# A two-block transformer on one core: first projections from the unnormalised input, convolution from PSUM, values ahead of logits, merged sums kept in PSUM

## The reference, cut to what matters

```
h     = rmsnorm(x, ln_mix_pre)                      # x * rs(token) * gain(feature)
proj  = h @ w_in
qkv   = silu(depthwise_conv5(proj[q,k,v of GDN]))   # 5 taps over tokens, 3*1024 channels
q, k  = l2norm(q), l2norm(k)                        # 8 heads of 128
g, b  = decays and betas from 32 gate columns
o_a   = rmsnorm(delta(q,k,v,g,b) + reversed delta) * silu(z)
o_b   = dilated window attention, 3 groups x 4 heads, joined by softmax over groups
merged= sigmoid(ga) * (o_a @ w_branch_a) + sigmoid(gb) * (o_b @ w_branch_b)
x     = x + rmsnorm(merged @ w_out);  x = x + rmsnorm(relu(rmsnorm(x) @ w_ff1)**2 @ w_ff2)
```

## Time and profile before

| | |
|---|---|
| median of 3 runs | 2108.91 us (2108.44 to 2112.96) |
| the profiled execution | 2110.14 us |
| its span | 2108.3 us |
| TensorE busy | 1998.5 us, 95% |
| VectorE, ScalarE, GpSimd busy | 940.0, 743.6, 614.7 us |
| TensorE's share of the chain that ended last | 86% (DVE 7%, ACT 4%) |
| mean granted clock | 0.972 |

### The profile page before, as it was taken

How to read it: one execution, slowest core, us unless ns; L and a number is a source line. 1 busy time by engine, 2 the same in 40 slices (tenths; PEclk the granted TensorE clock), 3 DMA queues, 4 the chain that set the end, 5 groups by cost and what they waited for, 6 DMA issues and landing times.

```text
span 2108.3 us, 25286 instructions
## 1 busy us (share of the span) xinstructions
PE 1998.5 (95%) x10748; PEld 1607.1 (76%) x10748; DVE 940.0 (45%) x1549; ACT 743.6 (35%) x1235; POOL 614.7 (29%) x206
## 2 busy tenths in 40 slices
PE   6998899999999999999999999998999999999997
PEld 3777899999977787778778888887766548766456
DVE  4797455656522221303336403514534664434663
ACT  4674232221433322322233212223343553343551
POOL 2431211222432322334424444442423002423001
PEclk8999799999999999999999999998999999999999
DMA  4121000000233322322222222221312002212001
GB/s 170 60 80 60 1 1 2 2 1 1 95 120 105 106 90 76 111 84 91 89 80 82 98 100 100 100 99 61 130 60 80 1 1 83 90 60 80 1 1 40
DMA packets 29001, 142.01 MB, mean 67 GB/s; under 512 B 2871, under 2 KB 7351, under 8 KB 14808
## 3 DMA queue, kind: packets, MB, share of 16 engines
q1 hardware_dynamic: 18944, 123.27, 16.5%
q10 hardware_dynamic: 9944, 17.12, 2.5%
HBM read 135.13 MB, written 5.24 MB: 67 GB/s over the span
## 4 chain that ended last, share of the span: by engine, by line
PE 86%; DVE 7%; ACT 4%; issue 1%; DMA 0%; POOL 0%; SPq 0%; POOLq 0%; DVEq 0%; ACTq 0%
PE bank L398 48%; PE bank L942 13%; PE bank L599 4%; PE bank L409 3%; PE bank L1800 3%; PE bank L1821 3%; PE bank L1807 2%; DVE WK L868 2%; PE bank L957 2%; PE bank L1275 1%; DVE WK L887 1%; PE bank L1251 1%; PE bank L1749 1%; ACT WK L1930 1%; ACT w_part L356 1%
## 5 line engine op out<-in xcount | busy, mean ns | idle before, releaser
L398 PE MATMUL bank<-x_part,w_part 128*128 128x512 f32 x3360 | 786.7, 394 | 3.5 <-ACT WK L1497 3.0
L398 PEld LDWEIGHTS bank<-x_part,w_part 128*128 128x128 f32 x3360 | 633.1, 189 | 141.5 <-issue 9.0
L2240 POOL TENSOR_TENSOR w_part<-RAW,w_part 128x2048 fp32r<-128x2048 f32 (+1 forms) x90 | 403.3, 4484 | 780.1 <-ACT w_part L356 777.7
L942 PE MATMUL bank<-WK 128*128 128x64 f32 (+1 forms) x2336 | 281.2, 277 | 3.4 <-DVE WK L1088 1.6
L942 PEld LDWEIGHTS bank<-WK 128*128 128x128 f32 x2336 | 275.7, 195 | 4.3 <-DVE WK L1088 1.8
L2240 POOL TENSOR_TENSOR w_part<-WK,w_part 128x2048 fp32r<-128x2048 f32 (+1 forms) x30 | 126.2, 4206 | 376.5 <-ACT w_part L356 376.5
L356 ACT ACTIVATE w_part<-RAW 128x2048 fp32r<-128x2048 f32 (+1 forms) x90 | 166.4, 1850 | 173.9 <-PE bank L398 138.3
L398 PE MATMUL bank<-f_part,w_part 128*128 128x512 f32 x768 | 174.4, 389 | 0.0
L398 PEld LDWEIGHTS bank<-f_part,w_part 128*128 128x128 f32 x768 | 144.2, 188 | 29.9
L868 DVE SCALAR_TENSOR_TENSOR WK<-WK,COL 128x512 f32<-128x512 f32 x96 | 101.7, 1060 | 3.4
L1009 ACT ACTIVATE WK<-bank 128x256 f32<-128x256 f32 x80 | 31.0, 388 | 200.9 <-PE bank L957 200.6
(11 more groups left out here) (257 smaller groups left out, 2372.6 us busy)
## 6 DMA issues: line engine op xcount, KB each, us to landing
RAW<-wts SPq DMA_DIRECT2D x84, 1024.0 KB, 4.8
WK<-wts SPq DMA_DIRECT2D x24, 1024.0 KB, 4.8
WK<-scratch ACTq DMA_DIRECT2D x16, 256.0 KB, 2.7
RAW<-wts SPq DMA_DIRECT2D x6, 512.0 KB, 3.3
WK<-wts SPq DMA_DIRECT2D x6, 512.0 KB, 3.2
scratch<-WK ACTq DMA_DIRECT2D x4, 768.0 KB, 3.3
WK<-xT SPq DMA_DIRECT2D x4, 512.0 KB, 7.1
WK<-xT ACTq DMA_DIRECT2D x1, 2048.0 KB, 11.1
```

Source lines behind the costliest of these rows:

```text
L398: mm = pe.eng.matmul(b[:, :], W[w][:, k, c:c + P], src[x][k], start=start and k == 0 and n == 0, stop=stop and k == kn - 1 and n == 2)
L942: mul = lambda o, a, b: E.matmul(o, a, b, start=True, stop=True)
L2240: eng.tensor_tensor(low_part(i), raw_part(i), high_part(i).bitcast(F32), ALU.subtract).then_inc(w_split, 1)
```

## The change

Four places are rewritten.

- **Front.** VectorE first forms x * gain alone, in two parts (`UX`, called `gained_part`), as x arrives. TensorE takes the four tiles of chunk 0 from it, in pairs: the high weight piece by both parts, then the low piece. The row factor rs is multiplied into these four banks afterwards (`rowed`, in place). The gate projection moves behind tile (1, 0). ScalarE rounds weight piece 0 before the norm's Ln, piece 1 after its Exp and piece 2 behind the second rounded activation tile. The gate weights are loaded behind weight piece 0. On the engines the gates' small steps come about two tiles later.
- **Convolution.** `XP` is gone. ScalarE writes the middle tap times its weight to `CV`, and VectorE adds four taps read from the bank, 510 or 511 wide; the bank is free only then.
- **Dilated order.** The first value projection stands before the first two logits, and the third and fourth logits before the first `av`, behind the transposes of the values. VectorE copies the values before it handles the third logits.
- **Merge.** The stage barrier on TensorE goes, with explicit waits in its place. ScalarE takes the first two sigmoids inside the dilated stage. The products with WB and the sum stay in the bank; rounding and subtraction read the bank, and the subtraction of tile i - 1 stands behind the sum of tile i.

```diff
 def act_norm(...):
+            ahead(upto=1)
             for k in range(KO):
                 ...
                 act.eng.activation(XH[0][:, k, :], norm_mem(nm)[2][:, k % 2, :], ACT.Copy)...
+                if k == 1:
+                    ahead(upto=2)
 def load_pe():
             pe_norm("n1")
+            for p in range(2):
+                bs = [job(("qkv", 0, 2 * p + j)) for j in range(2)]
+                hi, lo = (w.rearrange("p (k n) -> p k n", n=256) for w in (high_part(p), low_part(p)))
+                pe.wait_ge(*at(("hi", p)))
+                for k in range(KO):
+                    pe.wait_ge(*at(("ux", k)))
+                    for j, b in enumerate(bs):
+                        for x in range(2):
+                            pe.eng.matmul(b[:, :], hi[:, k, j * P:(j + 1) * P], UX[x][:, k, :], start=k == 0 and x == 0, stop=False)
+                pe.wait_ge(*at(("split", p)))
+                for j, b in enumerate(bs):
+                    for k in range(KO):
+                        mm = pe.eng.matmul(b[:, :], lo[:, k, j * P:(j + 1) * P], UX[0][:, k, :], start=False, stop=k == KO - 1)
+                    mm.then_inc(*pe.did(("pe", ("qkv", 0, 2 * p + j))))
+                used(p)
 def load_act():
-            act_norm("n1", XT, need=arrived, before_sum=lambda: ahead(upto=1))
+            act_norm("n1", XT, need=lambda k: [(x_in[k // 2], 16)], before_sum=lambda: ahead(upto=0))
 def load_dve():
+            for k in range(KO):
+                dve.wait_ge(x_in[k // 2], 16)
+                g = col("ln_mix_pre", k)
+                dve.eng.tensor_scalar(UX[0][:, k, :], XT[:, k, :], g, None, ALU.mult).then_inc(*dve.did())
+                dve.wait_ge(*dve.last())
+                dve.eng.scalar_tensor_tensor(out=UX[1][:, k, :], in0=XT[:, k, :], scalar=g, in1=UX[0][:, k, :].bitcast(F32),
+                                             op0=ALU.mult, op1=ALU.subtract).then_inc(*dve.did(("ux", k)))
 def qkv_pe():
-            for c in range(6):
+            for c in range(1, 6):
                 for i in range(4):
-                    fm(("qkv", c, i), f"A{c}", i * P, HTS)
-                    if c == 0 and i == 1:
+                    fm(("qkv", c, i), f"A{c}", i * P, HTS, **(dict(need=lambda k: ("n1", "h", k)) if c == 1 and i == 0 else {}))
+                    if c == 1 and i == 0:
+                        gates_project_pe()
+                    if c == 1 and i == 1:
                         gates_turn_pe()
-                    if c == 1 and i == 0:
+                    if c == 1 and i == 3:
                         gates_sum_pe()
-                    if 1 <= c <= 4 and i == 1:
+                    if 1 <= c <= 4 and i == (2 if c == 1 else 1):
                         sums(c - 1)
 def qkv_act():
-                act.eng.activation(XP[:, n % 2, 2:S + 2], ps(("qkv", c, i))[:, :], ACT.Copy)\
-                    .then_inc(*act.did(("xp", n), free=("qkv", c, i)))
+                act.eng.activation(CV[:, n % 2, :], ps(("qkv", c, i))[:, :], ACT.Copy, scale=col("conv", n * CONV + 2))\
+                    .then_inc(*act.did(("cv", n)))
 def qkv_dve():
+            def rowed(i):
+                dve.wait_ge(*at(("pe", ("qkv", 0, i))))
+                V.tensor_tensor(ps(("qkv", 0, i))[:, :], ps(("qkv", 0, i))[:, :], RSB, ALU.mult)...
-                V.tensor_scalar(cv, XP[:, n % 2, 0:S], wc(0), None, ALU.mult).then_inc(*dve.did())
-                for j in range(1, CONV):
-                    dve.wait_ge(*dve.last())
-                    V.scalar_tensor_tensor(out=cv, in0=XP[:, n % 2, j:j + S], scalar=wc(j), in1=cv, ...
+                for j, (to, at_, m) in ((0, (2, 0, S - 2)), (1, (1, 0, S - 1)), (3, (0, 1, S - 1)), (4, (0, 2, S - 2))):
+                    if j:
+                        dve.wait_ge(*dve.last())
+                    V.scalar_tensor_tensor(out=cv[:, to:to + m], in0=x[:, at_:at_ + m], scalar=wc(j), in1=cv[:, to:to + m], ...
+                                           free=("qkv", c, i) if j == CONV - 1 else None))
 def dil_pe():
+                project(hh, "v", 0)
                 for label in [("bqk", hh, g) for g in range(6)]:
                     pe.wait_ge(*at(label))
                 logits(n)
                 logits(n + 1)
-                for g in range(3):
-                    project(hh, "v", g)
+                project(hh, "v", 1)
+                project(hh, "v", 2)
                 turn(n)
                 turn(n + 1)
-                logits(n + 2)
                 ...
+                logits(n + 2)
+                logits(n + 3)
                 for t in range(TT):
                     pe.wait_ge(*at(("bvc", hh, t)))
                 av(n)
-                logits(n + 3)
                 av(n + 1)
 def dil_act():
+            for i in range(2):
+                act.wait_ge(*at(("pe", ("GA", 0, i))))
+                A.activation(SG[:, i, :], ps(("GA", 0, i))[:, :], ACT.Sigmoid)...
+            ahead("GA0", 0)
 def merge_pe():
-            pe.stage("merge")
+            pe.stage("merge", barrier=False)
 def merge_act():
-                    act.eng.activation(MG[0][:, 4 * half + i, :], TM[:, i, :], ACT.Copy)...
+                    act.eng.activation(MG[0][:, 4 * half + i, :], ps(("WB", half, i))[:, :], ACT.Copy)...
 def merge_dve():
+            def low(half, i):
+                dve.wait_ge(*at(("mgh", half, i)))
+                V.tensor_tensor(MG[1][:, 4 * half + i, :], ps(("WB", half, i))[:, :], MG[0][:, 4 * half + i, :].bitcast(F32), ALU.subtract)...
-                    V.tensor_tensor(SG[:, i, :], ps(("WB", half, i))[:, :], SG[:, i, :], ALU.mult)...
-                    V.tensor_tensor(TM[:, i, :], TM[:, i, :], SG[:, i, :], ALU.add)...
-                for i in range(4):
-                    ...
-                    V.tensor_tensor(MG[1][:, 4 * half + i, :], TM[:, i, :], MG[0][:, 4 * half + i, :].bitcast(F32), ALU.subtract)...
+                    V.tensor_tensor(m, m, SG[:, i, :], ALU.mult).then_inc(*dve.did())
+                    dve.wait_ge(*dve.last())
+                    V.tensor_tensor(m, m, TM[:, i, :], ALU.add).then_inc(*dve.did(("mg", half, 1, i)))
+                    if i:
+                        low(half, i - 1)
+                low(half, 3)
```

More of the change, by code:

```diff
@@ L628, in build @@
         GF = wk(19712, S)
+        UX = parts("gained_part", 22784, KO, S)
         def load_pe():
@@ L829, in qkv_act @@
                 act.wait_ge(*at(("pe", ("qkv", c, i))))
-                act.wait_ge(*at("xpzero"))
+                if not c:
+                    act.wait_ge(*at(("rowed", i)))
                 if n >= 2:
-                    act.wait_ge(*at(("conv", n - 2)))
-                act.eng.activation(XP[:, n % 2, 2:S + 2], ps(("qkv", c, i))[:, :], ACT.Copy)\
-                    .then_inc(*act.did(("xp", n), free=("qkv", c, i)))
+                    act.wait_ge(*at(("si", *tiles[n - 2])))
+                act.eng.activation(CV[:, n % 2, :], ps(("qkv", c, i))[:, :], ACT.Copy, scale=col("conv", n * CONV + 2))\
+                    .then_inc(*act.did(("cv", n)))
                 if i % 2:
@@ L856, in qkv_dve @@
             dve.stage("qkv")
[L857 to L869 removed]
+            RSB = norm_mem("n1")[1]
@@ L1397, in dil_act @@
                         bias_tiles(r)
-                for r in range(2):
-                    prob(n + r)
-                    bias_tiles(n + r + 2)
                 if not hh:
@@ L1412, in dil_act @@
                         ahead(f"Bv{hh}", (g - 1) * 2 * P)
+                    else:
+                        for r in range(2):
+                            prob(n + r)
+                            bias_tiles(n + r + 2)
                 moves(n)
@@ L1420, in dil_act @@
             moves(15)
+            for i in range(2):
+                act.wait_ge(*at(("pe", ("GA", 0, i))))
+                A.activation(SG[:, i, :], ps(("GA", 0, i))[:, :], ACT.Sigmoid).then_inc(*act.did(("sg", 0, 0, i), free=("GA", 0, i)))
+            ahead("GA0", 0)
         def dil_dve():
@@ L1484, in merge_pe @@
                 for nm, src in (("GA", HTS), ("WA", tiles_of(OAT, KO)), ("GB", HTS), ("WB", tiles_of(OBT, 4))):
+                    if nm == "WA" and half == 0:
+                        pe.wait_ge(*at(("end", "zgate", "act")))
+                        pe.wait_ge(*at(("end", "zgate", "dve")))
+                    if nm == "WB" and half == 0:
+                        pe.wait_ge(*at(("end", "dil", "dve")))
                     for i in range(2 if nm == "GA" and half == 0 else 0, 4):
@@ L1492, in merge_act @@
                 for m, nm in enumerate(("GA", "GB")):
-                    for i in range(4):
+                    for i in range(2 if not m and not half else 0, 4):
                         act.wait_ge(*at(("pe", (nm, half, i))))
@@ L1504, in merge_act @@
                     act.wait_ge(*at(("mg", half, 1, i)))
-                    act.eng.activation(MG[0][:, 4 * half + i, :], TM[:, i, :], ACT.Copy).then_inc(*act.did(("mgh", half, i)))
```

(5 more changed lines are left out.)

58 lines of the change are left out of this document (29 added, 29 removed).

## The result

The changed kernel takes 2061.03 us (median of 4 runs, 2060.73 to 2062.03), the kernel before 2108.77 us (4 runs, 2108.44 to 2112.96). The ratio is 0.977, its 95% interval 0.9753 to 0.9787. The profiled execution of the changed kernel took 2060.84 us with a span of 2059.0; the one of before had 2108.3.

The account below looks back on a forecast made before the run. TensorE was taken to bound the kernel, with stops and half-rate clock to remove. Front 27.2, dilated order 16.6 and merge 6.4 sum to 50.2, from 2110.14 to 2059.9; the runs' median 1.2 lower gave 2059, range 2050 to 2075.

Parts of the forecast that it names:

- the way to the second sums: Front, up to the end of the second chunk's sums: about 91.3 us instead of 111.92, -20.6.
- the periods: Front's steady part, four tiles each: 26.64 us falls to 23.7; two periods give -5.9.
- The start: Front: TensorE starts chunk 0 at about 15.9 us, after the first weight piece's high part.
- The wait near 60 us: Front: TensorE waits 4.4 us from about 61, for the convolution of tile (1, 0) at 65.3.
- bound "without any fall 22.9": Front, up to the second chunk's sums: gain of 22.9 instead of 20.6 if the clock never falls.
- the range of the parts: Whole kernel: 2052 to 2069 us, from the bounds of the front, dilated stage and merge.
- The tail: End of the front: one last convolution takes 2.9 us instead of 3.6, -0.7.
- The mechanism of the front: Convolution taps: two SBUF operands wait for GpSimd's whole instruction, a bank and one SBUF operand do not.
- rival A: Convolution: taps from a bank still wait for GpSimd, periods stay 26.6, 5.9 and 4 lost, 2069 us; chance 8%.
- The dilated order: Dilated stage, k to next q: 30.8 and 32.1 us become 27.3, twice each, -16.6.
- Rival B: Dilated stage: the clock falls in each hh behind the transposes, 4 x 1.7 us, 2066; chance 10%.
- The merge: Merge: -4.5 us from the first sigmoids' stop and its clock fall, -1.9 at the end, together -6.4.

Follow-up runs that it names:

- the taps alone: The changed kernel with the old front, chunk 0 again projected from the normalised input, taps still read from the bank: 2072.7 us.
- the start alone: The changed kernel with ScalarE copying each tile to SBUF and the four taps reading and adding there, chunk 0 still early: 2083.94 us.
- three such orders on ScalarE: The changed kernel with gate steps behind the last square, values' last rounding behind probability copies, merged parts' roundings before the next weight piece: 2053.46 us.

## Why the prediction was right, point by point

The forecast was 2059, range 2050 to 2075; it came to 2061.03. The sum of 50.2 stands against 49.3 in the span. It hides two mis-sized terms, the way to the second sums and the periods, and that they cancel is luck.

- **The start.** Forecast 15.9, by the first weight rounding; it was 17.07, by the norm's row sums, which stand ahead on TensorE and last 10.03. I had not looked at who releases whom there. In the other profiled executions with this start those sums take 8.6 to 10.1, and chunk 0 starts between 15.75 and 17.4. The gate parts were ready before GpSimd's first subtraction, so VectorE met two of them and not three and the last activation part was ready at 40.6, not 42.3.
- **The wait near 60 us and the way to 91.3.** The wait was to end at 65.4, by ScalarE, and ended at 66.0, by ScalarE. It lasted 2.1 and not 4.4 because TensorE came to it at 63.9 and not at 61: a later start, and three sums of 0.86 each where I had counted half. From there I had 0.4 for the last sum, two falls of the clock at 1.7, gate sums 4 and the chunk's sums 1.7; measured were 1.13, no fall, 2.6 and 3.5. Hence 89.75 and -22.2 instead of -20.6. The missing falls are luck: four of the seven profiled executions have both, two have one. The bound "without any fall 22.9" covers it, but the terms as written give 20.6 + 3.4 = 24.0. The same care was missing in the range of the parts: their bounds give 2053.7 to 2070.4, not 2052 to 2069.
- **The periods: the step that failed.** I took "1.7 of sums" for a period, half of what they cost. Four sums take 3.43 (0.86 each, two passes of 0.43). So the period of before, 26.64, held a stop of 1.4 and not 3.1; the new period is 25.24, and two give -2.8 instead of -5.9. The tail: -0.6 for the rest of the stage. Front: 25.6 at the last tile, 27.2 forecast.
- **The mechanism of the front** was right in that taps on a bank don't wait for GpSimd (748 ns; I had taken 692). But the text reads as if the start were the gain and the taps worth 5.9. The two experiments show 13.8 for the taps alone, and 2.6 for the start alone. Had rival A (the taps still wait) been true, the cost, going by the kernel with the taps from SBUF, would have been up to 23, not the 10 I gave it: 2084, outside my range.
- **The dilated order.** -16.6 forecast, -15.9 measured. 27.52 per hh against 27.3; the bank behind ScalarE's rounding was next late, as forecast, and taking it away gave the 26.9 of bare work. Rival B is out: by the rule of the Trainium skill ("TensorE: Matmul & The Clock Gate", "Part 4: PE-mode transpose") `av` would run at half clock behind the transposes; it took 2.68 for 24 in each hh, and the granted clock is 1.00 from 636 to 645 us.
- **The merge.** -6.4 forecast, -7.1 at the end of the projection and -6.2 with the slower L547. The low parts came at 997.6, 999.5 and 1001.5, which is 1045.1, 1047.1 and 1049.0 with the 47.5 between the two kernels there added; forecast were 1045.2, 1047.4, 1049.5. I had taken 1.9, between 1.1 (the work) and 2.8 (with the fall of the clock); it was 2.8: 1.4 for the six matmuls that now lie inside the stop, and the fall of before, which is gone. The first stop gave 2.9 and, in this pair of profiles, 1.45 of clock.
- **Waiting for GpSimd.** That a VectorE step with two SBUF inputs waits for GpSimd, and one with a bank and an SBUF input does not, is shown three times over: 7.36 against 3.12 for four taps in one kernel, 6.10 for eight taps beside GpSimd, 4.61 against 0.69 for the subtraction. The Trainium skill, "SBUF — State Buffer", "SBUF: two separate sides", names the same condition for its exclusive lock, two SBUF inputs; these rows agree, and in them an output in SBUF doesn't count: the taps and the low parts are written there.
- **Not foreseen:** -1.6 at the bias rows, +0.9 at L547, both clock, both in code that the change leaves alone.

## What to carry to other kernels

Ask of an earlier start who can keep up with it: with VectorE waiting for GpSimd, 20 us of head start were worth 2.6, and 11.7 once a tap read its bank. Then price a rival as a whole run, with every meeting of the two engines, not as the stop it brings back once. And when a stop is left, look for what stands ahead of the late step on its own engine; three such orders on ScalarE gave 7.9 us more. Last, before calling a stage's gain measured, look at more than one execution: here the same front ended anywhere between 89.75 and 93.2.

## What the runs showed of the hardware

- A VectorE step with one operand in a bank and a scalar from a column of SBUF takes 0.75 (L901, and L725 at 0.75 with both operands in SBUF); with an immediate scalar it takes 0.69 (L1474). I had priced the taps by the immediate one.
- An in-place VectorE product or sum on a bank takes 0.69 to 0.70 (L889, L1573, L1575), and ScalarE can round from the same bank right behind it.
- The clock falls or does not behind the same stop, in the same code. A stop of 2.1 was followed by full clock in one execution and by 0.64 in another; a stop of 2.97 by 143.2 for 624 matmuls in one kernel and 141.7 in the other. Behind the stop of 2.1, six of seven profiled executions show a fall. Most falls cost 1.3 to 1.7, the one at 1004.9 us with the joining sums in SBUF 2.8. So the stop is a sure gain, and the clock a likely one.
- A float32 matmul of 512 columns shows as two passes of 0.43. At the very start, under loads of 427 GB/s, its passes came 0.86 apart (the first five to eight of sixteen) though the granted clock reads 1.00. Why isn't settled; it sets the start of the projections.
